# Expert weights in pieces of two row tiles by 1024 columns, activations in 1024-column steps, and a first expert block of its own

## The reference

```python
def swiglu(h, w_gate, w_up, w_down):
    return (jax.nn.silu(h @ w_gate) * (h @ w_up)) @ w_down

def moe_swiglu(h, router, w_gate, w_up, w_down):      # h: 256 tokens x 1024
    logits = (t @ router).astype(jnp.float32)
    top_v, top_i = lax.top_k(logits, TOP_K)           # 2 of 8 experts
    w = jax.nn.softmax(top_v, axis=-1)
    combine = jnp.sum(jax.nn.one_hot(top_i, N_EXPERTS, dtype=jnp.float32) * w[..., None], axis=1)
    for e in range(N_EXPERTS):                        # w_gate[e], w_up[e]: 1024 x 3584; w_down[e]: 3584 x 1024
        out = out + combine[:, e:e + 1].astype(t.dtype) * swiglu(t, w_gate[e], w_up[e], w_down[e])
    return out.reshape(B, S, D)
```

## Time and profile before

| | us |
|---|---|
| three runs | 1549.84, 1548.06, 1545.35 |
| median | 1548.06 |
| span of the profiled execution, first to last instruction | 1548.7 |
| busy: PE | 1512.6 (98%) |
| busy: DVE | 1179.1 (76%) |
| busy: ACT | 964.8 (62%) |
| busy: POOL | 30.4 (2%) |

### The profile page before, as it was taken

One profiled execution on the slowest core, in us unless ns is written; L12 is line 12 of the kernel. 1 busy time (PEld: TensorE's weight loads), 2 busy tenths in 40 slices (PEclk: granted clock), 3 DMA queues, 4 the chain that ended last, 5 costly groups with the idle time before them and its releaser, 6 DMA issues.

```text
span 1548.7 us, 20199 instructions
## 1 busy us (share of the span) xinstructions
PE 1512.6 (98%) x7799; PEld 1296.3 (84%) x7799; DVE 1179.1 (76%) x900; ACT 964.8 (62%) x772; POOL 30.4 (2%) x43
## 2 busy tenths in 40 slices
PE   7889999999999989999999999999999999999998
PEld 7879999988888878888888888888888888888887
DVE  7764544456643579889888888988888988888987
ACT  4844433344453447767767776776776776776775
POOL 2100000001100000000000000000000000000000
PEclk9999999999996979999999999999999999999999
DMA  9445555553521539989999999999999999999994
GB/s 339 154 153 177 187 190 190 186 187 117 202 83 42 177 126 360 355 301 371 377 353 327 380 369 333 370 367 332 370 371 324 365 382 328 363 376 338 363 371 159
DMA packets 220012, 434.37 MB, mean 280 GB/s; under 512 B 6961, under 2 KB 9121, under 8 KB 219969
## 3 DMA queue, kind: packets, MB, share of 16 engines
q1 hardware_dynamic: 219504, 433.11, 79.0%
q0 software_dynamic: 368, 0.63, 0.1%
q10 hardware_dynamic: 96, 0.03, 0.0%
HBM read 432.69 MB, written 1.05 MB: 280 GB/s over the span
## 4 chain that ended last, share of the span: by engine, by line
PE 95%; DVE 2%; ACT 2%; issue 1%; DMA 0%; SPq 0%; POOL 0%; DVEq 0%
PE ps L673 25%; PE ps L674 24%; PE ps L675 24%; PE ps L687 4%; PE ps L690 4%; PE ps L689 4%; PE ps L970 2%; PE ps L986 2%; PE ps L979 1%; PE ps L850 1%; PE ps L840 0%; DMA raw<-in_lru_w_in_dram 0%; ACT whi L421 0%; PE ps L852 0%; PE ps L854 0%
## 5 line engine op out<-in xcount | busy, mean ns | idle before, releaser
L1055 DVE TENSOR_TENSOR wlo<-raw,whi 128x2048 fp32r<-128x2048 f32 x408 | 930.5, 2291 | 238.9 <-ACT whi L421 238.0
L421 ACT ACTIVATE whi<-raw 128x2048 fp32r<-128x2048 f32 x408 | 781.3, 1916 | 296.8 <-PE ps L675 217.2
L673 PE MATMUL ps<-whi,hT_hi 128*128 128x512 f32 x1056 | 415.6, 394 | 5.3 <-DVE hT_lo L1155 4.3
L674 PE MATMUL ps<-wlo,hT_hi 128*128 128x512 f32 x1056 | 413.8, 392 | 0.0
L675 PE MATMUL ps<-whi,hT_lo 128*128 128x512 f32 x1056 | 413.4, 391 | 0.0
L673 PEld LDWEIGHTS ps<-whi,hT_hi 128*128 128x128 f32 x1056 | 200.1, 190 | 48.2 <-DVE hT_lo L1155 4.5
L675 PEld LDWEIGHTS ps<-whi,hT_lo 128*128 128x128 f32 x1056 | 199.9, 189 | 42.2
L674 PEld LDWEIGHTS ps<-wlo,hT_hi 128*128 128x128 f32 x1056 | 200.0, 189 | 41.1
L673 PE MATMUL ps<-whi,aT_hi 128*128 128x512 f32 x448 | 179.1, 400 | 0.0
L675 PE MATMUL ps<-whi,aT_lo 128*128 128x512 f32 x448 | 175.1, 391 | 0.0
L674 PE MATMUL ps<-wlo,aT_hi 128*128 128x512 f32 x448 | 174.6, 390 | 0.0
(11 more groups left out here) (268 smaller groups left out, 1137.7 us busy)
## 6 DMA issues: line engine op xcount, KB each, us to landing
raw<-in_moe_w_up_dram SPq DMA_DIRECT2D x112, 1024.0 KB, 6.7
raw<-in_moe_w_gate_dram SPq DMA_DIRECT2D x111, 1024.0 KB, 6.6
raw<-in_moe_w_down_dram SPq DMA_DIRECT2D x111, 1024.0 KB, 6.8
raw<-in_fox_w_in_dram SPq DMA_DIRECT2D x16, 1024.0 KB, 5.5
raw<-in_ffn_w_gate_dram SPq DMA_DIRECT2D x14, 1024.0 KB, 5.1
raw<-in_ffn_w_up_dram SPq DMA_DIRECT2D x14, 1024.0 KB, 5.1
raw<-in_ffn_w_down_dram SPq DMA_DIRECT2D x14, 1024.0 KB, 5.0
raw<-in_lru_w_in_dram SPq DMA_DIRECT2D x8, 1024.0 KB, 11.5
```

The lines of the kernel that those rows point to most:

```text
L421: nc.scalar.activation(whi[:, m % HR], src, ACT.Copy).then_inc(hi_done, 1)
L673: mm(dst(t), hi, whi[:, m % HR, k], start=first and k == 0, stop=False)
L674: mm(dst(t), hi, wlo[:, m % HR, k], start=False, stop=False)
L1055: nc.vector.tensor_tensor(wlo[:, m % HR], src, whi[:, m % HR].bitcast(F32), ALU.subtract).then_inc(lo_done, 1)
```

## The change

It has four parts.

- A weight unit of the experts is 1 MB as before, but of two row tiles by 1024 columns (four by 512 where only 512 columns are left). The list of 42 units is a table, `EXPERT`, with (matrix, first row tile, row tiles, first column, width); a row piece in memory is 4 KB and not 2 KB.
- The hidden width is done in four steps p of 1024, 1024, 1024 and 512 columns (`PAIRS`, `PAIR_W`), with four gate, four up and four down units a step (two in the last). Silu, multiply, transposes (eight), copy and subtraction run on 1024 columns at once. Gate results take banks 4 and 5 together, up results 2 and 3, transposes 6 and 7; no second set is left. Under one pair of row weights TensorE does three matmuls for the left 512 columns and then three for the right ones. A down unit has two row tiles and all 1024 output columns.
- TensorE's first block is written out apart, without scatter; VectorE's first block has no accumulate, and the zeroing on GpSimd goes. TensorE reads the number of blocks after the first block.
- The transposes of the one-hot (L1014) move from the second step to a place right behind the scatter; ScalarE's copy of them (L643) moves with them.

Memory for the wider activations is found by laying them over the normalised tokens, which are no longer needed then; `m_scat` becomes two semaphores.

```diff
+PAIRS = 4
+PAIR_W = [2 * CW, 2 * CW, 2 * CW, CW]
+PAIR_U = [w // CW * 2 for w in PAIR_W]
+def expert_table():
+    units, first = [], {}
+    def half(matrix, p):
+        first["GU"[matrix], p] = len(units)
+        width = PAIR_W[p]
+        tiles = UK * CW // width
+        for n in range(PAIR_U[p]):
+            units.append((matrix, n * tiles, tiles, p * 2 * CW, width))
+    def down_rows(p):
+        first["D", p] = len(units)
+        for n in range(PAIR_U[p]):
+            units.append((2, p * 2 * UK + 2 * n, 2, 0, D))
+    for p in range(PAIRS):
+        half(0, p)
+        half(1, p)
+        if p:
+            down_rows(p - 1)
+    down_rows(PAIRS - 1)
...
 @block.sync
             def expert_load(i, b, e):
-                w, rows, col = units[i]
-                src = w[bass.ds(e, 1), rows * P:(rows + UK) * P, col * CW:(col + 1) * CW].rearrange(
+                matrix, row, tiles, col, width = EXPERT[i]
+                src = expert_w[matrix][bass.ds(e, 1), row * P:(row + tiles) * P, col:col + width].rearrange(
                     "o (k p) n -> p (o k) n", p=P)
...
 @block.scalar
-                for c in range(FC):
-                    if c == 1:
-                        hi_to(6, b)
-                        act.wait_ge(m_TS, at(1, 1, b))
-                        nc.scalar.activation(ST[:], ps[:, 7, 0:T], ACT.Copy).then_inc(m_ST, 1)
-                        act_T_hi(b, 0)
-                    hi_to(base(c) + 3, b)
-                    act.wait_ge(used, at(N_MOE + base(c) + 2, FFN_UNITS, b))
-                    act.wait_ge(m_act, at(max(c, 1), FC, b))
-                    nc.scalar.activation(gt[:, c % 2], ps[:, 4 + c % 2], ACT.Silu).then_inc(m_silu, 1)
-                    if c:
-                        hi_to(base(c) + 6, b)
-                        act_T_hi(b, c)
+                hi_to(3, b)
+                act.wait_ge(m_TS, at(1, 1, b))
+                nc.scalar.activation(ST[:], ps[:, 0, 0:T], ACT.Copy).then_inc(m_ST, 1)
+                for p in range(PAIRS):
+                    hi_to(last_of("G", p) + 2, b)
+                    silu(b, p, first)
+                    hi_to(last_of("U", p) + 3, b)
+                    act_T_hi(b, p)
...
 @block.tensor
+            def expert_unit(b, i, src, bank, first, last):
+                tiles, width = EXPERT[i][2], EXPERT[i][4]
+                slot = (N_MOE + i) % HR
+                pe.wait_ge(lo_done, at(N_MOE + i + 1, FFN_UNITS, b))
+                for k in range(tiles):
+                    hi, lo = src(k)
+                    for h in range(width // CW):
+                        cols = slice(k * width + h * CW, k * width + (h + 1) * CW)
+                        mm(ps[:, bank + h], hi, whi[:, slot, cols], start=first and k == 0, stop=False)
+                        mm(ps[:, bank + h], hi, wlo[:, slot, cols], start=False, stop=False)
+                        ins = mm(ps[:, bank + h], lo, whi[:, slot, cols], start=False, stop=last and k == tiles - 1)
+                ins.then_inc(used, 1)
+            def expert_block(b, first=False):
+                gather(b)
+                pe.wait_ge(m_xh, at(1, 1, b))
+                if not first:
+                    pe.wait_ge(m_ylo, at(0, 1, b))
+                    pe.wait_ge(m_ST, at(0, 1, b))
+                    for j in range(2):
+                        scatter(j)
+                selection_transposes()
+                pe.wait_ge(m_xl, at(1, 1, b))
+                for p in range(PAIRS):
+                    if p or not first:
+                        pe.wait_ge(m_silu, at(p, PAIRS, b))
+                    for n in range(PAIR_U[p]):
+                        half_unit(b, "G", p, n, 4)
+                        if p == 1 and n == 0:
+                            act_transposes(b, 0)
+                    if p or not first:
+                        pe.wait_ge(m_act, at(p, PAIRS, b))
...
+                    for n in range(PAIR_U[p]):
+                        half_unit(b, "U", p, n, 2)
...
+                    for d in ([p - 1] if p else []) + ([p] if p == PAIRS - 1 else []):
+                        pe.wait_ge(m_tlo, at(d + 1, PAIRS, b))
+                        for n in range(PAIR_U[d]):
+                            down_unit(b, d, n)
+                            if n == 0 and d < PAIRS - 1:
+                                act_transposes(b, d + 1)
             pe.wait_ge(hn_hi_done, 2)
+            expert_block(0, first=True)
             pe.wait_ge(blocks, 1)
             nblk = pe.value_load(nblk_i[0:1, 0:1], min_val=E, max_val=2 * E)
-            with pe.Fori(0, nblk) as b:
...
+            with pe.Fori(1, nblk) as b:
+                expert_block(b)
 @block.vector
-                accumulate(b)
-                for c in range(FC):
-                    lo_to(base(c) + 5, b)
-                    dve.wait_ge(used, at(N_MOE + base(c) + 4, FFN_UNITS, b))
-                    dve.wait_ge(m_silu, at(c + 2, FC, b))
-                    nc.vector.tensor_tensor(act_s[:, c % 2], gt[:, c % 2], ps[:, 2 + c % 2], ALU.mult
+                if not first:
+                    accumulate(b)
+                for p in range(PAIRS):
+                    n = PAIR_W[p]
+                    lo_to(last_of("U", p) + 2, b)
+                    dve.wait_ge(used, at(N_MOE + last_of("U", p) + 1, FFN_UNITS, b))
+                    dve.wait_ge(m_silu, at(p + 1, PAIRS, b))
+                    nc.vector.tensor_tensor(act_s[:, 0:n], gt[:, 0:n],
+                                            ps[:, 2:4].rearrange("p b n -> p (b n)")[:, 0:n], ALU.mult
                                             ).then_inc(m_act, 1)
-                    lo_to(base(c) + 6, b)
-                    act_T_lo(b, c)
-                    if c == 2:
+                    lo_to(last_of("U", p) + 3, b)
+                    act_T_lo(b, p)
+                    if p == 0:
                         dve.wait_ge(m_TS, at(1, 1, b))
-                        one_hot(bass.ds(b + 1, 1), at(3, 2, b))
+                        one_hot(bass.ds(b + 1, 1), at(2, 2, b))
```

More of the change, by code:

```diff
@@ L180, in hybrid_trunk @@
         with ExitStack() as a4:
-            hn = sb("hn", [P, TT, D], where=a4)
+            with ExitStack() as h4:
+                hn = sb("hn", [P, TT, D], where=h4)
+                gb = sb("gb", [P, D], where=h4)
+            with ExitStack() as t4:
+                aT_hi = sb("aT_hi", [P, 2, 2 * UK, P], F32R, where=t4)
+                aT_lo = sb("aT_lo", [P, 2, 2 * UK, P], F32R, where=t4)
+            sb("aT_home", [P, 4 * D], where=a4)
             hn_hi = sb("hn_hi", [P, TT, D], F32R, where=a4)
             hn_lo = sb("hn_lo", [P, TT, D], F32R, where=a4)
[L184 to L188, removed]
+            gt = sb("gt", [P, 2 * CW], where=a4)
+            act_s = sb("act_s", [P, 2 * CW], where=a4)
             S = sb("S", [P, TT, P], F32R, where=a4)
@@ L672, in tokens_unit @@
                         hi, lo = src(k0 + k, t)
-                        mm(dst(t), hi, whi[:, m % HR, k], start=first and k == 0, stop=False)
-                        mm(dst(t), hi, wlo[:, m % HR, k], start=False, stop=False)
-                        ins = mm(dst(t), lo, whi[:, m % HR, k], start=False, stop=last and k == UK - 1)
+                        mm(dst(t), hi, whi[:, m % HR, k * CW:(k + 1) * CW], start=first and k == 0, stop=False)
+                        mm(dst(t), hi, wlo[:, m % HR, k * CW:(k + 1) * CW], start=False, stop=False)
+                        ins = mm(dst(t), lo, whi[:, m % HR, k * CW:(k + 1) * CW], start=False, stop=last and k == UK - 1)
                 ins.then_inc(used, 1)
@@ L980, in scatter @@
                                  start=q == 0, stop=q == 1)
-                ins.then_inc(m_scat, 1)
-            def act_transposes(b, c):
-                pe.wait_ge(m_act, at(c + 2, FC, b))
-                for a in range(4):
-                    ins = nc.tensor.transpose(ps[:, 6, a * P:(a + 1) * P], act_s[:, c % 2, a * P:(a + 1) * P], ident[:])
-                ins.then_inc(m_T, 1)
-            def moe_unit(b, i, src, k0, bank, first, last):
-                tokens_unit(N_MOE + i, b, src, k0, 1, lambda t: ps[:, bank], first, last)
@@ L992, in of_xg, with selection_transposes, act_transposes @@
-            def of_xg(k, t):
-                return xg_hi[:, k], xg_lo[:, k]
+                ins.then_inc(m_scat[j], 1)
+            def selection_transposes():
+                for t in range(TT):
+                    ins = mm(ps[:, 0, t * P:(t + 1) * P], S[:, t], ident_r[:], start=t == 0, stop=True,
+                             skip_group_check=True)
+                ins.then_inc(m_TS, 1)
+            def act_transposes(b, p):
+                pe.wait_ge(m_act, at(p + 1, PAIRS, b))
+                for a in range(PAIR_W[p] // P):
+                    ins = nc.tensor.transpose(ps[:, 6 + a // 4, a % 4 * P:(a % 4 + 1) * P], act_s[:, a * P:(a + 1) * P],
+                                              ident[:])
+                ins.then_inc(m_T, 1)
@@ new lines, in half_unit, with down_unit @@
```

(12 more changed lines are left out.)

111 lines of the change are left out of this document (48 added, 63 removed).

## The result

| | before | changed |
|---|---|---|
| median of 6 runs each on one chip, us | 1547.66 | 1558.09 |
| lowest to highest | 1543.94 to 1549.84 | 1551.26 to 1560.04 |
| span of the profiled execution | 1548.7 | 1555.7 |

The ratio is 1.006 with a 95% interval of 1.0047 to 1.0073: slower by 9.3 us, between 7.3 and 11.3. The forecast was slower, 1555.5 us. Five of the six changed runs took 1557.5 to 1560.0 us at a mean granted clock of 0.977 or 0.978, and the one of 1551.26 us had 0.982.

The account below looks back on a forecast made before the run. TensorE was taken as the bound (122.9 of 123.3 us a block). Steady blocks +7.7, head -1.6 and tail +1.3 sum to +7.4 us on the span, 1555.5 us on the median; range 1547 to 1562.

Parts of the forecast that it names:

- A: Three wide steps a block: transposes wait for the longer VectorE multiply, 0.24 us each, 0.72 us a block.
- B: Expert unit behind the longer silu: its weight load is late by 0.19 us, losing 0.08, three times 0.24 a block.
- C: Fourth unit behind the transposes, held by the longer copy: late 0.16 us, losing 0.05, 0.15 a block.
- four sets and not seven: Activation transposes in a steady block: three sets fewer at 0.05 us each save 0.15 us a block.
- head: First block: earlier gather, no empty scatter, count read hidden, half the lead lost to the clock: -1.6 us once.
- tail: After the last unit: both halves of the last down-product end together, so X additions end later, +1.3 us once.
- Hidden as costed: Weight loads in steady blocks: 4 KB rows cost nothing, since nothing waits for a landing.
- The margins hold (1): Rival: no stalls in steady blocks, only the head shows, 1546.6 us; within 0.3% of before, chance 0.27.
- A faster rhythm by two banks (2): Rival: alternating banks under one pair of row weights shortens the matmul rhythm, about 1501 us; chance 0.11.
- Slower fetches (3): Rival: 4 KB rows are fetched slower; 5% less rate costs +50 us, giving 1606; chance 0.03.
- A falling clock (4): Rival: nine TensorE pauses a block lower the clock in steady blocks, 12 us, giving 1567; chance 0.03.

Follow-up runs that it names:

- trans_late: The changed kernel with the wide steps' transposes one unit later, copy and subtraction two conversions later: 1550.07 us in one run, steady block 123.58 us.
- copy_late: The changed kernel with the wide steps' copy of transposed activations and its subtraction one weight conversion later: 1557.46 us in one run, steady block 124.31 us.
- silu_late: The changed kernel with ScalarE's silu behind one more weight conversion: 1557.23 us in one run, steady block 124.10 us.
- all_mended: The changed kernel with silu_late, trans_late and tail_halves together: 1545.50 us against 1547.17 for the kernel before, ratio 0.9982.
- peel_only: The kernel before with only the first block written out apart, without scatter or accumulate, block count read behind it: 1547.29 us against 1548.25, ratio 0.9989.
- tail_halves: The changed kernel with a block's last two down units by column halves, as in the kernel before: 1556.54 us in one run, tail 4.45 us.
- mult_twice: The kernel before with each 512-wide VectorE multiply issued twice, first into a spare tile: 1567.63 us in one run, steady block 125.45 us.
- table_early: all_mended with a two-column silu on a spare tile ahead of the expert part, to load the table there: 1545.27 us against 1548.22, ratio 0.9978.

## Why the prediction came out as it did

The sign, the places and the mechanism were right; the size was 2.5 us short of the +9.9 of the account. By its steps (a block, unless said):

| step | forecast | measured | from |
|---|---|---|---|
| A, transposes behind the multiply | +0.72 | +0.73 | trans_late less copy_late |
| B, unit behind the silu | +0.24 | +0.43 | silu_late |
| C, fourth unit behind the transposes | +0.15 | +0.22 | copy_late |
| four sets and not seven | -0.15 | -0.12, the moved one-hot transposes in it | all_mended against before |
| sum | +0.96 | +1.26 (1.24 in the trace) | |
| head, once | -1.6 | -1.48 | peel_only |
| tail, once | +1.3 | +1.45 | tail_halves |

**A** was the term most at risk, priced from another place's restarts, and it held to a hundredth. Had the wide step as such cost the time (two banks, one set of them, fewer overlaps), halving the multiply would have changed nothing; it gave all of A back at its three places (0.72, of which 0.1 was lost again elsewhere), and mult_twice made the same wait in a kernel with no wide step at all.

**B is the term that was mis-sized.** The forecast took one place, in a later step, and multiplied by three. There it was near: lateness 0.20 (0.19 forecast), loss 0.10 (0.08). In the first step of a block the load is 0.28 late and the two units together lose 0.21; 0.10 + 0.10 + 0.21 is the 0.41 seen in the unit distances. The 0.08 by which the first step is later come from the silu's own start. It runs 0.28 us after the first matmul behind the last gate unit, and in the later steps 0.20 after it:

```profile
816.89 0.39 PE L1048 MATMUL ps<-whi,hT_hi 128*128 128x512 f32 x1
...
817.17 1.03 ACT L676 ACTIVATE gt<-ps 128x1024 f32<-128x1024 f32 x1 [0.88 <-PE ps L1050]
...
840.09 0.39 PE L1048 MATMUL ps<-whi,hT_hi 128*128 128x512 f32 x1
...
840.29 1.03 ACT L676 ACTIVATE gt<-ps 128x1024 f32<-128x1024 f32 x1 [0.87 <-PE ps L1050]
```

From there both take the same 5.21 to the weight load (817.17 to 822.38, 840.29 to 845.50). The kernel before had it too and the forecast could have read it there: in its steady blocks the first silu starts 0.28 behind that matmul, the others 0.20.

```profile
813.07 0.39 PE L673 MATMUL ps<-whi,hT_hi 128*128 128x512 f32 x1
...
813.35 0.60 ACT L648 ACTIVATE gt<-ps 128x512 f32<-128x512 f32 x1 [0.88 <-PE ps L675]
```

What holds the first silu back these 0.08 us is not shown.

**C** was an estimate from a lateness of 0.16 and lost 0.07 and not 0.05 each. Small errors, but each eight times: B and C are 0.26 a block, 2.1 of the 2.5 us.

**Head.** The gather's early start and the uncovered copy came as described. In the changed kernel the first expert matmul is 8.65 us after the one-hot and the clock rises 4.7 us behind it (5.0 forecast, 5.1 in peel_only; 4.7 to 5.1 in the nine kernels with the peeled block). That a 512-wide matmul is what the rise follows was an assumption, and no run tests it: the low stretch lasts 20.48 us in all eleven traces and ends 13.3 to 13.8 us after the one-hot. The read of the count is hidden. By the Trainium skill (TensorE: Matmul & The Clock Gate, section on architectural detail), whose rule is a queue 64 instructions deep, it should be, and peel_only agrees: its block 1 starts 2.72 us after the last unit of block 0 does, as in the other blocks. What the forecast missed in the first block is the table load: before, the slack took in most of its 1.28 us (two units of 2.83 and 2.90, 0.29 lost); with the wide silu behind it the weight load is 0.8 us late and 0.67 is lost (all_mended). That is nearly 0.4 us, once. It doesn't show in the total, because the forecast missed something on the other side as well: the two one-hot transposes, now right ahead of the first unit, fall into its wait. Gather and transposes together take 8.48 us in all_mended where the gather alone with its wait takes 8.45 in peel_only, which has the transposes later, for about 0.25. And the clock, measured from the one-hot, rose 0.40 sooner in the changed kernel than in peel_only, which is worth 0.20.

**Tail**: +1.45, shown by giving it back; the operations took their forecast order, copies as a pair (1.09), subtractions as a pair (1.29), scatters, additions.

**Hidden as costed**: nothing waits for a landing, though the median from issue to landing went from 6.6 to 6.8 us up to 7.0 to 7.2. The wider rows are not shown to be the reason: peel_only, with rows of 2 KB, has 7.0 to 7.1, and all_mended, with 4 KB in most units, 6.0 to 6.9. The changed kernel:

```profile
raw<-in_moe_w_down_dram SPq DMA_DIRECT2D x112, 1024.0 KB, 7.2
raw<-in_moe_w_gate_dram SPq DMA_DIRECT2D x111, 1024.0 KB, 7.0
```

**The rivals.** The margins hold (1): no, 72 waits say otherwise; as an order written otherwise it is all_mended, and 1545.5 us is close to the 1546.6 computed for it. A faster rhythm by two banks (2): no (the 12.9 us in its sum should be 12.1, 1555.5 less 1543.4; its 3 ns stand); matmuls in the steady units still start every 0.227 us (845.84 to the next at 846.07) and all_mended's unit is 2.72. Slower fetches (3): no, above. A falling clock (4): no, 1.00 in every steady block in spite of nine pauses each; the swing of which the Trainium skill (TensorE: Matmul & The Clock Gate, section on a second HAM failure mode) warns was not seen in any run here.

## What to carry to other kernels

Where the engine that sets the pace waits for engines that are 62% and 76% busy, halving the number of their operations by doubling each was a loss here, and with the order mended it gained only the 0.12 us a block at TensorE's own transposes: what counts is the slack between each small operation and the load that waits for it, 0.2 to 0.3 us here, and a doubled operation spends it. Work through the order of every helper engine around each widened operation, in every step and not in one; then move the consumer or the operation by one place, which cost nothing here and turned +0.6% into -0.2%. A stall of TensorE costs less than the lateness of the weight load, because that load had been 0.23 us ahead of its matmul; of this it got back about 0.1 before 512-wide matmuls and 0.17 before transposes.

## What the runs showed of the hardware

- A late weight load costs TensorE less than its lateness, because matmul and load then start together. Before a 512-wide stream, late 0.20 lost 0.10, and late 0.28 lost about 0.2: 0.16 at the restart (0.05 and 0.11) and the rest in the ten matmuls behind it, which start 0.231 apart and not 0.227. Before eight transposes, late 0.41 lost 0.24.
- A lead gained at a clock of 0.50 is worth half of itself at 1.00: 3.23 us at the first expert matmul became 1.48 at block 1 (peel_only). The clock's rise hardly moved. It came 13.31 us after the one-hot in the two kernels with the empty scatter and 13.36 to 13.76 in the nine without. The first 512-wide matmul didn't move much either: it was the empty scatter's, 8.34 after the one-hot before, and an expert unit's, 8.65, in the changed kernel. So these runs don't tell what the rise follows.
- A load of the silu table on ScalarE takes 1.28 us at whatever place the first silu has (565.68 us before, 566.71 changed, 572.63 in silu_late, 543.47 in table_early), and the silu follows it at once (572.63 + 1.28, then 573.93).
- The profiled executions differ ahead of the expert part, not in it: the steady blocks of one trace lie within 0.13 us of each other (within 0.04 before), while the second one-hot was ready anywhere from 545.4 to 548.5 us in the changed kernel and the variants with the same front.
